# A decoder block on one core: the modulation sums and the first projection taken by halves and steps, 32 turns into an unread bank ahead of the sums, and the weights' low parts made in quarters

## What is computed

```python
c_act = jax.nn.silu(c)
mod = (c_act @ ada_w[layer] + ada_b[layer])[:, None, :]
sh_m, sc_m, gt_m, sh_f, sc_f, gt_f = jnp.split(mod, N_MOD, axis=-1)
h = rms_norm(x, norm_g[layer, 0]) * (1 + sc_m) + sh_m
proj = h @ w_in          # q, kv_lat, q_idx, k_idx, w_idx, z, xbc, dt_raw, g_att, g_ssd
```

## Time and profile before

| what | us |
|---|---|
| median of 3 runs | 2447.12 (2447.07 to 2447.74) |
| the profiled execution | 2445.2 |
| its span, first to last instruction | 2443.5 |
| TensorE busy in the span | 2335.8 |
| VectorE / ScalarE / GpSimd busy | 1383.2 / 721.9 / 870.2 |

### The profile page before, as it was taken

The page is one execution under the profiler, slowest core; times in us unless marked ns, Lnnn a source line. Parts: engine busy times, 40 slices in busy tenths (PEclk is TensorE's granted clock), DMA queues, the critical chain, the costliest instruction groups (busy, mean ns, idle before and its releaser), DMA issues.

```text
span 2443.5 us, 31678 instructions
## 1 busy us (share of the span) xinstructions
PE 2335.8 (96%) x12022; PEld 1927.4 (79%) x12022; DVE 1383.2 (57%) x1956; ACT 721.9 (30%) x1360; POOL 870.2 (36%) x360
## 2 busy tenths in 40 slices
PE   3999999998999999999999999999999999999997
PEld 2977878884557988888877788899888888888886
DVE  4249999995657267685867565544632231322315
ACT  5144121105652234434365111034511211212112
POOL 1221233226671352634445233235323322333232
PEclk9999999999999999999999999999999999999999
DMA  7111452215652113141223443334211111111103
GB/s 270 36 35 39 151 181 90 99 61 177 206 165 72 40 61 125 50 141 40 85 102 125 148 145 133 120 104 138 87 52 52 46 40 51 51 51 34 51 34 78
DMA packets 144729, 230.25 MB, mean 94 GB/s; under 512 B 7956, under 2 KB 111732, under 8 KB 143604
## 3 DMA queue, kind: packets, MB, share of 16 engines
q1 hardware_dynamic: 119936, 166.11, 20.7%
q10 hardware_dynamic: 23684, 59.06, 6.3%
q0 software_dynamic: 1008, 3.67, 0.8%
HBM read 176.39 MB, written 52.43 MB: 94 GB/s over the span
## 4 chain that ended last, share of the span: by engine, by line
PE 71%; issue 12%; DVE 11%; ACT 3%; DVEq 1%; DMA 1%; ACTq 0%
PE ps L646 69%; DVE score L1703 2%; DVE score L1765 1%; DVE top L1761 1%; DVE c_out L1873 1%; DVE probT L1798 1%; DVE mod_sum L1641 1%; DVE x_tm L1980 1%; PE ps L865 1%; DVEq L1755 1%; PE ps L964 0%; PE ps L897 0%; DVE a_lo L1631 0%; ACT decay L1490 0%; DVEq L1763 0%
## 5 line engine op out<-in xcount | busy, mean ns | idle before, releaser
L646 PE MATMUL ps<-a_hi,w_hi 128*128 128x512 f32 x1728 | 679.0, 393 | 6.7 <-DVE k_idx_lo L1685 2.4
L646 PE MATMUL ps<-a_lo,w_hi 128*128 128x512 f32 x1728 | 674.8, 391 | 0.0
L576 POOL CAST w_hi<-raw 128x2048 fp32r<-128x2048 f32 x90 | 176.7, 1964 | 1276.2 <-PE ps L646 1045.0
L646 PE MATMUL ps<-a_hi,w_lo 128*128 128x512 f32 x1728 | 544.6, 391 | 0.0
L578 POOL TENSOR_TENSOR w_lo<-raw,w_hi 128x2048 fp32r<-128x2048 f32 x90 | 431.8, 4798 | 7.2
L2009 DVE TENSOR_TENSOR x_tm<-x_tm,ps 128x1024 f32<-128x1024 f32 x120 | 146.6, 1221 | 453.7 <-PE ps L646 453.1
L646 PEld LDWEIGHTS ps<-a_hi,w_hi 128*128 128x128 f32 x1728 | 325.4, 188 | 76.4 <-issue 3.0
L646 PEld LDWEIGHTS ps<-a_hi,w_lo 128*128 128x128 f32 x1728 | 325.4, 188 | 68.1
L646 PEld LDWEIGHTS ps<-a_lo,w_hi 128*128 128x128 f32 x1728 | 325.6, 188 | 65.8
L646 PE MATMUL ps<-w_hi,a_hi 128*128 128x256 f32 (+1 forms) x896 | 260.8, 291 | 8.5 <-ACTq L1547 4.8
L646 PE MATMUL ps<-w_lo,a_hi 128*128 128x256 f32 (+1 forms) x896 | 255.2, 285 | 0.0
(11 more groups left out here) (255 smaller groups left out, 3094.6 us busy)
## 6 DMA issues: line engine op xcount, KB each, us to landing
raw<-in_w_in_dram SPq DMA_DIRECT2D x35, 1024.0 KB, 5.3
ada_raw<-in_ada_w_dram SPq DMA_DIRECT2D x16, 1024.0 KB, 8.7
raw<-in_w_up_dram SPq DMA_DIRECT2D x16, 1024.0 KB, 5.7
raw<-in_w_down_dram SPq DMA_DIRECT2D x16, 1024.0 KB, 4.8
gates<-gate_d SPq DMA_DIRECT2D x12, 1024.0 KB, 4.9
act_raw<-acts_d ACTq DMA_DIRECT2D x20, 512.0 KB, 5.1
ada<-in_ada_w_dram SPq DMA_DIRECT2D x8, 1024.0 KB, 21.3
acts_d<-decay ACTq DMA_DIRECT2D x16, 512.0 KB, 3.9
```

The lines of the kernel that those rows point to most:

```text
L576: nc.gpsimd.tensor_copy(hi, src).then_inc(hi_made, 1)
L646: return nc.tensor.matmul(o, a, b, start=start, stop=stop)
```

## The change

- The sums: the last `ada_w` chunk is loaded and multiplied in two halves of 1024 columns, and `mod0_summed` is raised by each; TensorE waits for one half before its 8 products, then for the other. They go to bank 0 in place of 3.
- The gain: VectorE reads the sums in PSUM itself, with no copy by ScalarE. The part of the gain that needs no sum is made ahead.
- Turns: six tiles are turned before the sums, and banks 2 and 3 take two of them (`FIRST_TURN`). Behind them 32 further transposes of `x_tm` go to bank 1, which nobody reads.
- The first projection: for each k, a tile of turns and then the 12 matmuls of that k for token blocks 0 to 3, which wait only for tile k and for the quarter of `w_lo` that holds k; two more tiles' turns; then the same steps for blocks 4 to 7. The total of matmuls stays.
- The low parts: every split makes `w_lo` in four operations of a quarter of the columns, each of which raises `w_split`; all waits for `w_split` count four for one. Only the first block is used by its quarters.

```diff
--- before.py
+++ after.py
@@ -111,6 +111,7 @@
     N_OUT = N_O + 12
     N_MLP = N_OUT + 8
     NC = DFF // WC
+    LO_PARTS = 4
     N_ALL = N_MLP + 2 * NC
 
 
@@ -270,7 +271,7 @@
         mod0_summed = sem("mod0_summed")
         rows_turned, last_stored = sem("rows_turned"), sem("last_stored")
         c_ready = sem("c_ready")
-        mod0_done = sem("mod0_done")
+        ada_last = sem("ada_last")
         gain_ready = sem("gain_ready")
         squares = sem("squares")
         vars_ready = sem("vars_ready")
@@ -363,6 +364,8 @@
 
 
         FIRST_OUT = (5, 0, 1, 2)
+        IDLE_TURNS = 32
+        FIRST_TURN = (4, 5, 6, 7, 2, 3) + (4, 5, 6, 7) * 2 + (4, 5)
         FIRST_UP = ((0, 4, 2, 5), (1, 0, 3, 2))
         STEPS = 2 * NT
         UNITS = (0, 2, 1, 3)
@@ -375,14 +378,18 @@
                 s = n % 2
                 if n >= 2 or turn is not None:
 
-                    sp.wait_ge(w_split[s], n // 2 + (0 if turn is None else turn * (per // 2)))
+                    sp.wait_ge(w_split[s], (n // 2 + (0 if turn is None else turn * (per // 2))) * LO_PARTS)
                 dst = raw[s][:, :].rearrange(W3, c=WC) if dst is None else dst
                 sp.dma_start(dst, src).then_inc(raw_in[s], 16)
 
             for t in range(NT):
                 sp.dma_start(x_tm[:, t, :], x[0, t * P:(t + 1) * P, :]).then_inc(x_landed[t], 16)
             for k in range(KT):
-                sp.dma_start(ada0[:, k, :], ada_w[0, k * P:(k + 1) * P, 0:2 * D]).then_inc(ada_in[k], 16)
+                if k < KT - 1:
+                    sp.dma_start(ada0[:, k, :], ada_w[0, k * P:(k + 1) * P, 0:2 * D]).then_inc(ada_in[k], 16)
+            for half in range(2):
+                c = slice(half * D, half * D + D)
+                sp.dma_start(ada0[:, KT - 1, c], ada_w[0, D - P:D, c]).then_inc(ada_last if half else ada_in[KT - 1], 16)
             w = w_in[0]
             load(0, cols(w, C_KV))
 
@@ -575,7 +582,9 @@
                 src, hi, lo = raw[s][:, 0:width], w_hi[s][:, 0:width], w_lo[s][:, 0:width]
                 nc.gpsimd.tensor_copy(hi, src).then_inc(hi_made, 1)
                 pool.wait_ge(hi_made, n + 1 if turn is None else turn * per + (n + 1))
-                nc.gpsimd.tensor_tensor(lo, src, hi.bitcast(F32), ALU.subtract).then_inc(w_split[s], 1)
+                for j in range(LO_PARTS):
+                    c = slice(j * width // LO_PARTS, (j + 1) * width // LO_PARTS)
+                    nc.gpsimd.tensor_tensor(lo[:, c], src[:, c], hi[:, c].bitcast(F32), ALU.subtract).then_inc(w_split[s], 1)
 
             split(0)
             split(1, width=KT * NSM, landed=32)
@@ -640,7 +649,7 @@
                 return t[s][:, k * width + c0:k * width + c1]
 
             def w_wait(n, extra=0):
-                pe.wait_ge(w_split[n % 2], n // 2 + 1 + extra)
+                pe.wait_ge(w_split[n % 2], (n // 2 + 1 + extra) * LO_PARTS)
 
             def mm(o, a, b, start=False, stop=False):
                 return nc.tensor.matmul(o, a, b, start=start, stop=stop)
@@ -670,7 +679,7 @@
                         last = act_used(k, last)
                 return last
 
-            def tm_token(n, t, o, width, stationary=None, nk=KT, c0=0, wwidth=None, ks=None):
+            def tm_token(n, t, o, width, stationary=None, nk=KT, c0=0, wwidth=None, ks=None, half=None):
 
                 s = n % 2
                 sh, sl = stationary or (a_hi, a_lo)
@@ -678,9 +687,9 @@
                 for k in range(nk) if ks is None else ks:
                     r = slice(t * P, t * P + P)
                     wh, wl = (w_tile(w, s, k, c0, c0 + width, ww) for w in (w_hi, w_lo))
-                    mm(o, sh[:, k, r], wh, start=(k == 0))
+                    mm(o, sh[:, k, r], wh, start=(k == 0 and half != 1))
                     mm(o, sh[:, k, r], wl)
-                    last = mm(o, sl[:, k, r], wh, stop=(k == nk - 1))
+                    last = mm(o, sl[:, k, r], wh, stop=(k == nk - 1 and half != 0))
                 return last
 
             def norm_turn(j, tiles=range(2 * KT), banks=(4, 5, 6, 7)):
@@ -688,10 +697,12 @@
                 for i in tiles:
                     g, k = divmod(i, KT)
                     pe.wait_ge(normed, 8 * j + 4 * (g + 1))
-                    if i >= len(banks):
-                        pe.wait_ge(h_ready, 16 * j + i + 1 - len(banks))
+                    bank = banks[i % len(banks)]
+                    earlier = [e for e in range(i) if banks[e % len(banks)] == bank]
+                    if earlier:
+                        pe.wait_ge(h_ready, 16 * j + earlier[-1] + 1)
                     for t in range(4):
-                        last = nc.tensor.transpose(ps[:, banks[i % len(banks)], t * P:(t + 1) * P],
+                        last = nc.tensor.transpose(ps[:, bank, t * P:(t + 1) * P],
                                                    x_tm[:, 4 * g + t, k * P:(k + 1) * P], ident[:, :])
                     last.then_inc(turned, 1)
 
@@ -700,27 +711,30 @@
             pe.wait_ge(small_in, 16 * 6)
             nc.tensor.transpose(ps[:, 0, 0:112], rows_a[:, :], ident[0:112, 0:112])
             nc.tensor.transpose(ps[:, 1, 0:112], rows_b[:, :], ident[0:112, 0:112]).then_inc(rows_turned, 1)
-            norm_turn(0, range(4))
-            pe.wait_ge(mod0_summed, 1)
+            norm_turn(0, range(6), banks=FIRST_TURN)
+
+            for i in range(IDLE_TURNS):
+                nc.tensor.transpose(ps[:, 1, (i % 4) * P:(i % 4 + 1) * P], x_tm[:, i % 4, 0:P], ident[:, :])
             for m in range(2 * KT):
-                last = mm(ps[:, 3, m:m + 1], mod_sum[:, m * P:(m + 1) * P], ones[:, 0:1], start=True, stop=True)
-            last.then_inc(mod0_done, 1)
-            norm_turn(0, range(4, 12))
-
-            def kv_token(t):
-                return tm_token(0, t, ps[:, t // 2, (t % 2) * R:(t % 2) * R + R], R)
-
-            w_wait(0)
-            pe.wait_ge(h_split, KT)
-            kv_token(0)
-            norm_turn(0, (12, 13))
-            kv_token(1)
-            norm_turn(0, (14, 15))
-            kv_token(2)
-            kv_token(3)
-            pe.wait_ge(h_split, 2 * KT)
-            for t in range(4, NT):
-                last = kv_token(t)
+                if m % KT == 0:
+                    pe.wait_ge(mod0_summed, m // KT + 1)
+                last = mm(ps[:, 0, m:m + 1], mod_sum[:, m * P:(m + 1) * P], ones[:, 0:1], start=True, stop=True)
+            last.then_inc(c_ready, 1)
+
+            def kv_step(k, tokens):
+
+                pe.wait_ge(h_split, tokens[0] // 4 * KT + k + 1)
+                for t in tokens:
+                    last = tm_token(0, t, ps[:, t // 2, (t % 2) * R:(t % 2) * R + R], R, ks=(k,), half=t % 2)
+                return last
+
+            for k in range(KT):
+                norm_turn(0, (6 + k,), banks=FIRST_TURN)
+                pe.wait_ge(w_split[0], k * LO_PARTS // KT + 1)
+                kv_step(k, range(4))
+            norm_turn(0, (14, 15), banks=FIRST_TURN)
+            for k in range(KT):
+                last = kv_step(k, range(4, NT))
             last.then_inc(w_used[0], 1)
             w_wait(1)
             for t in range(NT):
@@ -1216,9 +1230,7 @@
             for t in range(NT):
                 nc.scalar.activation(x_tm[:, t, :], x_tm[:, t, :], ACT.Copy, scale=stat[:, NT + t:NT + t + 1]).then_inc(normed, 1)
 
-            act.wait_ge(mod0_done, 1)
-            nc.scalar.copy(mod[:, 0:16], ps[:, 3, 0:16]).then_inc(c_ready, 1)
-            norm_evac(0, 0)
+            norm_evac(0, 0, banks=FIRST_TURN)
 
             act.wait_ge(w_used[0], 1)
             for t in range(NT):
@@ -1641,18 +1653,28 @@
                     V.link(ve.scalar_tensor_tensor(mod_sum[:, :], ada0[:, k, :], c_act[:, k:k + 1], mod_sum[:, :], ALU.mult, ALU.add))
 
             dve.wait_ge(c_ready, 1)
+            V.link(ve.tensor_scalar(gain[:, 0:KT], vec_a[:, 8:16], 1.0, None, ALU.add))
+            V.link(ve.tensor_tensor(gain[:, 0:KT], gain[:, 0:KT], vec_a[:, 56:64], ALU.mult))
             mod_product(0)
             dve.wait_ge(squares, 1)
             ve.tensor_scalar(stat[:, 0:NT], stat[:, 0:NT], 1.0 / D, EPS, ALU.mult, ALU.add).then_inc(vars_ready, 1)
             dve.wait_ge(roots, 1)
             ve.reciprocal(stat[:, NT:2 * NT], stat[:, 0:NT]).then_inc(vars_ready, 1)
-            for k in range(1, KT):
+            for k in range(1, KT - 1):
                 mod_product(k)
-            dve.sem_inc(mod0_summed, 1)
+            for half in range(2):
+                if half:
+                    dve.wait_ge(ada_last, 16)
+                else:
+                    dve.wait_ge(ada_in[KT - 1], 16)
+                c = slice(half * D, half * D + D)
+                ve.scalar_tensor_tensor(mod_sum[:, c], ada0[:, KT - 1, c], c_act[:, KT - 1:KT], mod_sum[:, c],
+                                        ALU.mult, ALU.add).then_inc(mod0_summed, 1)
+
             dve.wait_ge(c_ready, 2)
-            V.link(ve.tensor_tensor(mod[:, 0:16], mod[:, 0:16], vec_a[:, 0:16], ALU.add))
```

(5 more changed lines are left out.)

## The result

| | before | changed |
|---|---|---|
| median, us | 2447.4 (2447.1 to 2448.0, 4 runs) | 2430.4 (2427.1 to 2434.3, 4 runs) |
| ratio, 95% interval | | 0.9931, 0.9913 to 0.9949 |
| profiled execution, us | 2445.2 | 2434.3 |
| its span, us | 2443.5 | 2432.5 |

The change makes the kernel faster by 17.1 us, or 0.69%. I forecast 7.0 less, 2440.0, within 2434.5 to 2445.0: the direction was right, the size and the range were wrong. The span of the profiled execution gained 11.0 us.

A forecast was written before the change was run, and what follows sets the result against it. TensorE was taken as the bound, busy 2335.8 of 2443.5 us, leaving only idle and slow time to win. The terms -7.0 - 1.9 + 0.8 + 1.1 = -7.0 took 2447.1 to 2440.0 us, range 2434.5 to 2445.0.

The forecast's parts named there:

- First stage: Up to the reading of the KV columns: an earlier gain and steps end it at 77.1 against 84.05, 7.0 us gained.
- Sums in halves: Modulation sums before the gain: eight of the 16 sums start 1.2 us sooner; sums done at 44.2 instead of 46.5.
- Quarters, everywhere else: All splits behind the first stage: longer GpSimd work is hidden and VectorE's savings and losses cancel, 0 within 4 us.
- The variance near 1337: VectorE's 8-column variance ends 3 us sooner beside a quarter, and the scalings behind it lose 1.1: -1.9 us.
- The state space stage: Its four groups: quarters save 1 us on the held state update and lose it on the next product: 0, within 1.5.
- Near 1662: Merge stage: a VectorE series ends later and SP's weight load is delayed beside the stores: +1.1 us, between 0 and +3.
- 1719.76: A VectorE series there, one product held 3.9 us before: with quarters the four operations end about 0.8 us later, +0.8.
- the second line: Sum of quarters' effects behind the first stage, -1.9 + 0.8 + 1.1, taken to lie between -4 and +4 us.
- The clock holds: Rival, first stage: the sums' passes keep the fast clock, so sums end at 41.8: -9.1, 2438 us; chance 0.18.
- Turns don't raise the clock: Rival, first stage: idle turns leave the clock low, so sums end at 45.8: -5.4, 2441.7 us; chance 0.12.
- Gain lost later: Rival: the merge stage's queue or a clock fall near 172 or 1346 gives back more than 3: 2445 us; chance 0.08.
- GpSimd becomes late: Rival, state space and merge stages: lengthened splits make TensorE wait for GpSimd, +20 in all, 2467 us; chance 0.05.

The follow-up runs named there:

- e1: The changed kernel run again with the same code: median 2425.4 us, ratio 0.9919.
- e3: The changed kernel with every low part made whole again, no quarters: median 2441.2 us, ratio 0.9976.
- e5: The changed kernel with quarters in the first two weight blocks only, whole low parts after: median 2442.2 us, ratio 0.9975.
- e2: The kernel before with only the quartered low parts added: median 2433.1 us, ratio 0.9947.
- e10: The changed kernel with whole low parts in the merge and output stages alone, quarters elsewhere: median 2438.7 us, ratio 0.9962.
- e9: The changed kernel with whole low parts in the MLP alone, quarters in every stage before it: median 2433.1 us, ratio 0.9932.
- e6: The changed kernel with quarters up to the state space stage and whole low parts from there: median 2439.1 us, ratio 0.9964.
- e7: The changed kernel with quarters in the first two and the late blocks, whole low parts between: median 2431.1 us, ratio 0.9929.
- e15: The changed kernel with 50 idle turns, x loads behind the merge's stores, and turns in the waits near 1340 and 1671 us: median 2424.3 us.
- e8: The changed kernel with the next loads of x held until the merge's stores have landed: median 2426.7 us, ratio 0.9912.
- e13: The changed kernel with 24 unread turns ahead of the merge wait near 1671 us: median 2430.1 us, ratio 0.9925.
- e14: The changed kernel with 24 unread turns ahead of each wait, near 1340 and 1671 us: median 2426.8 us, ratio 0.9913.
- e4: The changed kernel with 50 idle turns in place of 32: median 2424.1 us, ratio 0.9903.
- e18: e15 with low parts in eighths in place of quarters: median 2428.3 us, ratio 0.9930.

## Why the prediction was wrong

**First stage: right, by the medians and this profile.** Forecast 7.0 us, measured 6.4 in the profile of the changed kernel and 7.7 in e1's, and, by the medians, 6.5 in e3 (whole low parts everywhere) and 5.8 in e5 (whole behind the first stage) (each against the kernel before on the same chip). e3's profile has only 4.0 at the reading of the columns and nothing left at the end, so part of this agreement is luck. Sums in halves: the first 16 were to start at 38.3 and began at 39.31, of which 0.9 is that the whole profile runs later there (turns from 28.14 in place of 27.23). The turns quickened and ended at 36.0 (forecast 35.4). The clock was to fall at 39.3 and fell at about 38.2, so no pass ran fast: the sums ended at 46.3 in place of 44.2, and the gain with them. In e1's profile it fell at 40.6, and the 32 passes took 5.63 us where I had 5.9. The three small VectorE operations took 0.17 us each, as counted. What was lost on the sums came back in the steps: the first matmul ran at 49.4, and 28.3 us later the columns could be read, where I had 29.0.

**Quarters, everywhere else: the step that failed.** I had put it at 0, as -1.9 + 0.8 + 1.1, between -4 and +4. By the medians it is -14.5 alone (e2) and -15.7 beside the rest (e1 against e3). Point by point, in the profiles:
- The variance near 1337: forecast -1.9, measured -2.2 (e10 against e9, and the same between the kernel before and the changed one). Right.
- The state space stage: forecast 0. Two `zy` waits of 0.92 are gone, and each stretch is 0.8 shorter: -1.6; e6 against e5 gives 3.1 us by the medians. I had argued that a series gives back on its next product what it saves on the state update. It does, 0.85 for 0.80, but `zy`, for which TensorE waits, comes before the giving back.
- Near 1662: forecast +1.1. The profile reads -1.1, but a fall of the clock behind the wait for `row` that the kernel before has and this one hasn't accounts for 1.6 of it (the stretch takes 70.4 us in e1, where the clock fell, and 68.8 here). Where it fell in both, quarters cost 0.5 against the kernel before (70.4 in e1 against 69.9) and won 1.3 against e10 (70.5 in e9 against 71.9). So the sign isn't settled.
- 1719.76: forecast +0.8. Instead the wait of 1.14 us for `a_lo` behind it disappeared, and the stretch from the merge wait on took 2.0 less than before; but e9 and e10, with quarters and without, need 59.3 each, so that the quarters bring it isn't shown.

So the traces bear out that quarters shorten holds on TensorE's path, for some 4 to 5 us (e2's profiled span is 4.2 below the kernel before). The other ten of e2's 14.5 are in no trace. The experiments place most of them in the merge and output stages (e7, e10) and don't show the mechanism.

The changed kernel's span makes 11.0 in all against the forecast's 7.0. Without the first stage's 6.4 that is 4.6 for the second line, just past its bound of 4, and it includes falls of the clock that have nothing to do with quarters. What took the result out of the range is a part outside every profile of the changed kernel, some 6 to 8 us in five of its seven executions without one. The range had no term for it, and my rivals only had losses behind the first stage, never a gain.

**The two groups: cause open.** No execution without a profile leaves a trace. e15's profile, which is as short as its other executions, can be laid beside e1's, which is in the upper group: they agree to 0.1 us until 1247 us, and then e15 is 1.6 us quicker by the first wait's clock and 6.7 by the merge (122.6 us against 129.3 from the wait near 1599 to the one near 1725), where its last store landed within 5.9 us and TensorE turned for 1.9 us and idled for 0.8. The sum, 8.3, is near the distance of the groups, 2425 and 2433. That suggests that in the lower group the merge's stores land in time and the clock doesn't fall, and e5, e6 and e10, with whole low parts in those stages, show no lower group. But e15 is another kernel, with turns in the waits and the loads held back, and e8 speaks against it: its merge stretch took 124.6 us, and its profiled execution still took 2431.8.

A rival that no run tests is a sum of small falls. In some profiles the clock falls for about 3.4 us behind a short wait where in others it doesn't: near 147 us (the changed kernel, e10, e13; not e1, e15), near 564 us (the changed kernel, e5, e8; not e1, e15), behind the wait for `row` (before, e1, e10; not the changed kernel, e14). The first and the last cost 1.6 us each, and a few of them together are as large as the distance of the groups. Against any account by the clock stands that the executions of the kernel before take the same time with a mean granted clock of 0.986 and of 0.991.

**The rivals.** *The clock holds* came out for part of the sums in e4 (4.88 us for 32 passes), e1 (5.63) and e5 (5.31), and for nearly all in e18 (3.73 us), where more turns ended later; in the profile of the changed kernel it didn't. *Turns don't raise the clock* fell: 32 in 3.66 us. *Gain lost later*: 1.7 us behind 146, outweighed here, but in e3's profile all of it was lost. *GpSimd becomes late* did not happen with quarters and did with eighths. The chance of "faster" was also added up wrongly: three quarters of 0.57, most of 0.18 and half of 0.12 make about 0.65, not 0.75.

## What to carry to other kernels

When two engines exclude each other from the SBUF, look at how long the long instruction is and not only at how busy its engine is: cut it until the other engine's short operations on the critical path wait for a fraction of it, and stop before the cutting engine becomes late itself. Price such a change stage by stage, at each operation on which TensorE waits, and give "no net effect in a series" no zero of its own until every operation inside the series for which TensorE waits has been followed. Where the executions without a profile scatter more than those of the kernel before, the profiled one can be among the slow ones, and its landmarks then hold falls of the clock that another execution doesn't have. So compare a landmark in two profiles of the same kernel before giving its movement to the change.

## What the runs showed of the hardware

Turns (transposes of 128 columns) alone brought TensorE to 2.4 GHz: the last 32 of 56 took 0.114 us each. In e14 24 turns of the identity in each of two waits went with a granted clock of 1.00 throughout; in e13 as many turns in the second wait were followed by a fall to 0.50. During passes of one column it fell: with 50 turns ahead of them, in e4, it read 1.00 until 40 us and 0.50 from 42 us in the middle of the passes, at 0.152 us a pass on the mean; in e18, where they began 0.16 us behind the turns, 32 of them took 3.73 us.

The clock falls behind short waits of the same code in some executions and not in others. Behind the wait for `row`, 2.02 us long in both, it fell to 0.50 for 3.5 us in e1 and stayed at 1.00 in the changed kernel's profile, and the stretch to the merge wait took 70.4 us against 68.8.

A VectorE operation of 8 columns with its one input and its output in SBUF took 4.57, 1.25 and 0.70 us beside GpSimd's parts of 2048, 512 and 256 columns. The Trainium skill (SBUF — State Buffer, two separate sides) says that GpSimd and VectorE lock each other out until an instruction ends where VectorE's is in a 2-port mode, or has two SBUF inputs and GpSimd's reads SBUF. These three numbers agree with a hold until the end of GpSimd's part, if this operation runs in such a mode, which no trace names; and the three small operations with an operand in PSUM took 0.17 us each while GpSimd ran its quarters.
